# A two-layer trunk on one core: stick-breaking queries split unscaled out of PSUM, the norm factor of each token in the sigmoids

## The chip, the cores and the metric

The kernel runs on one core of one Trainium2 chip. The time is that of one execution on the device, in microseconds. Three runs of the kernel before gave 2856.43, 2856.97 and 2860.07 us, a median of 2856.97 us. The core has TensorE (matmuls, PE in the profile, its weight loads PEld), VectorE (DVE), ScalarE (ACT), GpSimd (POOL) and SyncE (SP), which work side by side and meet at semaphores. Each takes its instructions in the order in which they were written. TensorE writes to PSUM, which has 8 banks of 128 x 512 float32.

## The reference

Two layers, of which the first mixes tokens by a short convolution and the second by stick-breaking attention. The change is in the second alone. Cut to what matters there:

```python
h = rmsnorm(x, g_mix[i])                      # one factor per token: rsqrt(mean(x*x) + eps)
p0, p1, p2 = split(h @ w_in[i])               # queries, keys, values of 16 heads of 64
z = einsum(q, k) * 64 ** -0.5                 # keys before the query's own place only
log_keep = log_sigmoid(-z)
a = exp(log_sigmoid(z) + sum of log_keep over the later keys)
o = a @ v
```

The factor of a token multiplies all of its query. So it can be put on the query, or on the row of z that belongs to the query. The kernel works on sigmoids in place of logarithms: keep = sigmoid(-z), a running product of keep from the last key to the first, times sigmoid(z).

## The kernel before

Activations lie with features on the partitions and the 1024 tokens along the row. To keep float32 precision each operand of a large product is split into a rounded part (hi) and what is left (lo), and three matmuls are made of one (`three`, lines 1756 to 1758).

The stick-breaking layer goes head pair by head pair, 8 pairs. `pair` exists on every engine and has 8 items: item `it` is query block `t = it % 4` (256 tokens) of head `it // 4` of the pair. Two rows `r` of 128 queries make up an item. For one row TensorE computes z into banks 0 to 3 (`z`, lines 1985 to 1987, the last matmul of it adds the mask), ScalarE takes both sigmoids from there (lines 960 and 961), VectorE forms the running product (`scan`, line 1440), GpSimd multiplies the two (`weigh`, line 658). In the next item TensorE transposes the result into banks 4 and 5 (`turn`, line 2027), ScalarE and VectorE split it (lines 986 and 1482), and TensorE multiplies it with the values (`weighted`, lines 2043 and 2044). ScalarE and VectorE add up the two halves of the output (lines 1010 and 1528).

In the same loop TensorE computes the queries, keys and values of the next pair, `hp + 1`: six pieces of 8 steps of three matmuls, pieces 0 and 1 the query halves (tokens 0 to 511 and 512 to 1023), 2 and 3 the keys, 4 and 5 the values. All six go through one bank, number 7, one after the other (`project`, line 1989). The table `FILL` says how many steps stand behind each row of z and each part of `weighted`:

```python
FILL = [(3, 3), (2, 2, 2), (4, 1, 1, 1), (0, 2, 1, 1, 1), (3, 3), (2, 2, 2), (4, 2, 1, 1), (0, 4, 0, 0, 0)]
```

So piece 0 ends behind z of row 0 in item 1, `(1, 0)`, and piece 1 behind z of row 0 in item 2, `(2, 0)`. The first step of piece 2 stands right behind z of row 1 in item 2, and waits until bank 7 has been emptied. `ENDS` holds the six places, and VectorE empties the bank there (`project`, line 1442): for queries it multiplies with 1/8 and the norm factors R into the buffer `tf` (line 1456), for the rest with R alone (line 1236). Later ScalarE rounds `tf` into `sq` or `sk` (line 972) and VectorE subtracts (`lo_part`, line 1469). For the queries both stand at the end of items 1 and 2.

`head_place` gives the slots of `sq`: the first head of every pair has slot 0. So the queries of the next pair are written over those that this pair's items 0 to 3 read. z of item 3 is computed in item 2, and reads tokens 768 to 1023 of slot 0.

Pair 0 and pair 7 stand alone in the program, pairs 1 to 6 are a loop of three turns with two pairs each. Pair 7 has no projection in it.

Of the kernel before, what the change touches and what calls it, by code (L numbers as in the profile page):

```python
# [27 lines left out]
P = 128  # L28
# [57 lines left out]
def trunk(nc, xT, memT, wpack, vectors, out):  # L86
# [6 lines left out]
    for i in range(LAYERS):  # L93
# [3 lines left out]
        u, f, v = u + C_UNITS, f + C_UNITS, v + 2 * C_UNITS  # L97
# [13 lines left out]
    with ExitStack() as ctx:  # L111
# [50 lines left out]
        eps_r2 = place("eps_r2", [P, KB], F32)  # L162
        Z = cursor[0]
# [186 lines left out]
        zeros_made = sem("zeros_made")  # L350
        vT_full = sem("vT_full")
# [127 lines left out]
        assert len(ENDS) == 6  # L479
        ln = slice(0, HALF), slice(HALF, SEQ)  # L480
# [291 lines left out]
        def _(act):  # L772
# [101 lines left out]
            for i in range(LAYERS):  # L874
# [80 lines left out]
                else:  # L955
                    def sigmoids(row, par, r, t):
                        n = key_count(r, t)
                        act.wait_ge(z_full, row + 1)
                        z = banks(2 * r)[:, 0:n]
                        act.activation(keep[:, par, r, 0:n], z, ACT.Sigmoid, scale=-1.0).then_inc(keep_ready, 1)  # L960
                        act.activation(sig[:, par, r, 0:n], z, ACT.Sigmoid).then_inc(sig_ready, 1)  # L961

                    def project(hp, to, piece, b=7):

                        if piece < 4:
                            act.wait_ge(evacuated, hp * 6 + (v0 + piece + 1))
                            half = ln[piece % 2]
                            for other in range(1 + piece // 2):
                                for hh in range(2):
                                    slot, rows, twin = head_place(hh, to)  # L970
                                    dst = (sq, sk)[piece // 2]
                                    act.activation(dst[twin if other else rows, slot, half], tf[rows, half], ACT.Copy
# [16 lines left out]
                    def pair(hp, par, last, first=False):  # L989

                        for it in range(ITEMS):
# [3 lines left out]
                            if not (last and it == ITEMS - 1):  # L995
                                for r in range(2):
                                    sigmoids(hp * ROWS + (2 * (it + 1) + r), (it + 1) % 2, r, (it + 1) % 4)
                            if not last and it in (0, 3, 7):
# [13 lines left out]
                            if not last and it in (1, 2):  # L1012
                                project(hp + 1, 1 - par, it - 1)
# [7 lines left out]
                    act.wait_ge(x_spilled, 16)  # L1021
                    for r in range(2):
# [178 lines left out]
        def _(dve):  # L1201
# [107 lines left out]
            for i in range(LAYERS):  # L1309
# [124 lines left out]
                else:  # L1434
# [7 lines left out]
                    def project(hp, piece, b=7):  # L1442

                        part, h = piece // 2, piece % 2
                        if h == 0:
# [8 lines left out]
                        if part == 0:  # L1454

                            dve.scalar_tensor_tensor(tf[:, ln[h]], ps[:, b, :], float(SHEAD) ** -0.5,  # L1456
                                                     R[:, ln[h]], ALU.mult, ALU.mult).then_inc(evacuated, 1)
                        else:
                            scaled(tf[:, ln[h]], b, h)

                    def lo_part(hp, to, piece):
# [786 lines left out]
```

## Time and profile before

| | |
|---|---|
| three runs, median | 2856.97 us |
| the profiled execution, its own time | 2850.37 us |
| its span | 2848.8 us |
| busy: TensorE, VectorE, ScalarE, GpSimd | 2667.8, 1451.9, 1060.1, 590.7 us |
| stick-breaking stage | some 1394 to 2003 us of the span |
| one steady pair in it | 1484.05 to 1555.28 us, 71.2 us |
| mean granted clock of TensorE | 0.976 |

Busy times say which engine has most to do, and not what ends a wait. In a pipeline such as this stage the rows in time order, with the idle time in front of an instruction and what ended it, show where an engine stands still. Matmuls overlap in these rows: one of 512 columns is shown as 0.39 us long, and the next starts 0.23 us behind it. A granted clock of 1.00 is 2.4 GHz, 0.50 is 1.2 GHz.

### The profile page before, as it was taken

The numbers are of one execution on the slowest core, as the hardware profiler recorded it, in microseconds if no ns is written. First come the engines' busy times: TensorE is split into PE (matmuls) and PEld (weight loads), VectorE is DVE, ScalarE is ACT, GpSimd is POOL, SyncE is SP. The second block draws the span as 40 slices with busy tenths as digits, with TensorE's granted clock in tenths as the row PEclk, the third lists the DMA queues.
The fourth block names the chain that finished last, engine by engine and source line by source line (L and its number), as shares of the span: only waits on it lengthen the run. The fifth ranks groups of instructions, "written<-read, shape, count | busy, mean of one in ns | idle before, by whom it ended". The sixth has DMA issues, their size and how long they took to land.

```text
span 2848.8 us, 35436 instructions
## 1 busy us (share of the span) xinstructions
PE 2667.8 (94%) x12680; PEld 2220.0 (78%) x12680; DVE 1451.9 (51%) x1793; ACT 1060.1 (37%) x1749; POOL 590.7 (21%) x463
## 2 busy tenths in 40 slices
PE   7999999988999999999999889896998899999999
PEld 7888888866888878887877777775786788887887
DVE  7454434285444442334677767677328544444131
ACT  6450103243333330225666556565324333333020
POOL 2200000152222210003033333332015222221000
PEclk9999999999999999999999999998999999999999
DMA  6401111212222261103111101111321222226111
GB/s 200 141 30 44 52 52 45 88 52 89 89 103 103 77 231 51 43 34 140 54 29 30 31 23 30 30 30 61 127 88 52 103 81 96 103 81 228 51 51 69
DMA packets 57439, 221.77 MB, mean 78 GB/s; under 512 B 7280, under 2 KB 7280, under 8 KB 51824
## 3 DMA queue, kind: packets, MB, share of 16 engines
q1 hardware_dynamic: 43920, 164.68, 17.1%
q0 software_dynamic: 13120, 49.29, 5.1%
q10 hardware_dynamic: 288, 6.29, 0.5%
q8 instruction: 72, 1.18, 0.2%
q14 instruction: 39, 0.32, 0.0%
HBM read 170.43 MB, written 49.81 MB: 77 GB/s over the span
## 4 chain that ended last, share of the span: by engine, by line
PE 80%; DVE 7%; issue 5%; POOL 3%; ACT 3%; DMA 1%; POOLq 0%; SPq 0%; ACTq 0%; DVEq 0%
PE ps L1756 25%; PE ps L1758 24%; PE ps L1757 24%; POOL sig L658 2%; PE ps L2027 2%; ACT sig L961 1%; PE ps L1986 1%; PE ps L1985 1%; DVE x L1620 1%; DVE tile_lo L1629 1%; DVE w_lo L1208 1%; DVE tile_lo L1634 1%; DVE keep L1440 1%; DMA stage<-d_act 1%; PE ps L1857 1%
## 5 line engine op out<-in xcount | busy, mean ns | idle before, releaser
L1756 PE MATMUL ps<-xg_hi,w_hi 128*128 128x512 f32 x1280 | 517.2, 404 | 21.0 <-DVE tf L1456 8.4
L1757 PE MATMUL ps<-xg_lo,w_hi 128*128 128x512 f32 x1280 | 503.9, 394 | 0.0
L1758 PE MATMUL ps<-xg_hi,w_lo 128*128 128x512 f32 x1280 | 503.5, 393 | 0.0
L1756 PE MATMUL ps<-tile_hi,g_hi 128*128 128x512 f32 x1120 | 444.6, 397 | 55.6 <-DVE gate L1236 26.2
L1758 PE MATMUL ps<-tile_hi,g_lo 128*128 128x512 f32 x1120 | 441.0, 394 | 0.0
L1757 PE MATMUL ps<-tile_lo,g_hi 128*128 128x512 f32 x1120 | 439.4, 392 | 0.0
L1756 PEld LDWEIGHTS ps<-xg_hi,w_hi 128*128 128x128 f32 x1280 | 243.4, 190 | 74.2 <-DVE tf L1456 10.5
L1756 PEld LDWEIGHTS ps<-tile_hi,g_hi 128*128 128x128 f32 x1120 | 212.8, 190 | 103.0 <-issue 59.0
L1758 PEld LDWEIGHTS ps<-xg_hi,w_lo 128*128 128x128 f32 x1280 | 243.1, 190 | 53.5
L1757 PEld LDWEIGHTS ps<-xg_lo,w_hi 128*128 128x128 f32 x1280 | 243.8, 190 | 44.8 <-issue 0.7
L1756 PE MATMUL ps<-act_hi,d_hi 128*128 128x512 f32 x704 | 276.6, 393 | 0.0
L1758 PE MATMUL ps<-act_hi,d_lo 128*128 128x512 f32 x704 | 275.6, 392 | 0.0
L1757 PE MATMUL ps<-act_lo,d_hi 128*128 128x512 f32 x704 | 273.8, 389 | 0.0
L1639 DVE TENSOR_TENSOR g_lo<-quads,g_hi 128x512 fp32r<-128x512 f32 x200 | 178.9, 895 | 161.4 <-ACT g_hi L1109 161.3
L781 ACT ACTIVATE w_hi<-raw 128x1024 fp32r<-128x1024 f32 x104 | 109.8, 1058 | 398.4 <-PE ps L1758 389.9
L1758 PEld LDWEIGHTS ps<-tile_hi,g_lo 128*128 128x128 f32 x1120 | 212.5, 190 | 48.2
L1757 PEld LDWEIGHTS ps<-tile_lo,g_hi 128*128 128x128 f32 x1120 | 212.9, 190 | 46.3
L1208 DVE TENSOR_TENSOR w_lo<-raw,w_hi 128x1024 fp32r<-128x1024 f32 x104 | 139.4, 1341 | 178.2 <-ACT w_hi L781 176.4
L658 POOL TENSOR_TENSOR sig<-sig,keep 128x383 f32<-128x383 f32 (+3 forms) x121 | 167.0, 1385 | 267.2 <-DVE keep L1440 266.9
L1440 DVE TENSOR_TENSOR_SCAN keep<-keep 128x128 f32<-128x128 f32 (+7 forms) x128 | 181.7, 1433 | 52.6 <-ACT keep L960 51.9
L1715 DVE TENSOR_TENSOR x<-x,ps 128x512 f32<-128x512 f32 x64 | 43.3, 687 | 305.5 <-PE ps L1758 305.4
L1109 ACT ACTIVATE g_hi<-quads 128x512 fp32r<-128x512 f32 x200 | 125.1, 626 | 139.4 <-PE ps L1758 139.4
(212 smaller groups left out, 4130.9 us busy)
## 6 DMA issues: line engine op xcount, KB each, us to landing
raw<-wpack SPq DMA_DIRECT2D x104, 512.0 KB, 3.6
quads<-wpack SPq DMA_DIRECT2D x40, 1024.0 KB, 5.5
stage<-d_act POOLq DMA_DIRECT2D x44, 512.0 KB, 5.0
d_raw<-wpack SPq DMA_DIRECT2D x32, 704.0 KB, 4.1
d_act<-up SPq DMA_DIRECT2D x40, 256.0 KB, 2.1
d_act<-gate SPq DMA_DIRECT2D x40, 256.0 KB, 2.1
d_x<-x SPq DMA_DIRECT2D x16, 512.0 KB, 6.1
x<-d_x SPq DMA_DIRECT2D x16, 512.0 KB, 3.8
```

The source lines that it names most:

```text
L658: pool.tensor_tensor(sig[:, par, r, 0:n - 1], sig[:, par, r, 0:n - 1], keep[:, par, r, 1:n], ALU.mult).then_inc(a_ready, 1)
L781: act.activation(w_hi[s][:], raw[s][:], ACT.Copy).then_inc(w_hi_ready, 1)
L961: act.activation(sig[:, par, r, 0:n], z, ACT.Sigmoid).then_inc(sig_ready, 1)
L1109: act.activation(g_hi[i][q][:].rearrange("p (a c) -> p a c", a=1), granule_source(i, c % 2, q).rearrange("p (a c) -> p a c", a=1), ACT.Cop ...
L1208: dve.tensor_tensor(w_lo[s][:], raw[s][:], fp(w_hi[s][:]), ALU.subtract).then_inc(w_lo_ready, 1)
L1440: dve.tensor_tensor_scan(k, k, k, 1.0, ALU.mult, ALU.bypass).then_inc(scanned, 1)
L1639: dve.tensor_tensor(g_lo[i][q][:], granule_source(i, c % 2, q), fp(g_hi[i][q][:]), ALU.subtract).then_inc(g_lo_ready, 1)
L1715: dve.tensor_tensor(x[:, m, ln[h]], x[:, m, ln[h]], ps[:, (6 + 2 * m) % 8 + h, :], ALU.add).then_inc(x_added, 1)
L1756: pe.matmul(out, whi, mhi, start=start, stop=False, skip_group_check=chained)
L1757: pe.matmul(out, whi, mlo, start=False, stop=False, skip_group_check=chained)
L1758: return pe.matmul(out, wlo, mhi, start=False, stop=stop, skip_group_check=chained)
L2027: last = pe.transpose(ps[:, 4 + n % 2, j * P:(j + 1) * P], sig[:, it % 2, r, k * P:(k + 1) * P], ident[:])
```

## The change

The queries are no longer scaled. `R` and 1/8 go into `q_scale`, two columns per block of 128 tokens (+ and -), made once before the pairs by two VectorE instructions of 128 x 8. Both sigmoids take their scale from it, one number per query row, where they had a constant. For pieces 0 and 1 VectorE's multiplication into `tf` is gone: ScalarE rounds straight out of bank 7, and VectorE subtracts out of bank 7. Both now stand where `QUERIES` says: behind the sigmoids (ScalarE) and the scan (VectorE) of row 0 in item 1, and of row 1 in item 2. TensorE waits before pieces 1 and 2 for the subtraction, where it waited for the multiplication. The counts of `evacuated` follow from this (4 for a pair, not 6).

```diff
+        q_scale = place("q_scale", [P, 2, KB], F32)
...
+        QUERIES = {(1, 0): 0, (2, 1): 1}
...
-                        act.activation(keep[:, par, r, 0:n], z, ACT.Sigmoid, scale=-1.0).then_inc(keep_ready, 1)
-                        act.activation(sig[:, par, r, 0:n], z, ACT.Sigmoid).then_inc(sig_ready, 1)
+                        tok = 2 * t + r
+                        act.activation(keep[:, par, r, 0:n], z, ACT.Sigmoid, scale=q_scale[:, 1, tok:tok + 1]
+                                       ).then_inc(keep_ready, 1)
+                        act.activation(sig[:, par, r, 0:n], z, ACT.Sigmoid, scale=q_scale[:, 0, tok:tok + 1]
+                                       ).then_inc(sig_ready, 1)
...
                         if piece < 4:
-                            act.wait_ge(evacuated, hp * 6 + (v0 + piece + 1))
+                            if piece == 0:
+                                act.wait_ge(bank_full, hp * 3 + (f0 + 1))
+                            elif piece == 1:
+                                act.wait_ge(w_used, hp * 3 + (u0 + 1))
+                            else:
+                                act.wait_ge(evacuated, hp * 4 + (v0 + piece - 1))
...
-                                    act.activation(dst[twin if other else rows, slot, half], tf[rows, half], ACT.Copy
+                                    act.activation(dst[twin if other else rows, slot, half],
+                                                   ps[rows, b, :] if piece < 2 else tf[rows, half], ACT.Copy
                                                    ).then_inc(sqk_hi_ready, 1)
...
                                     sigmoids(hp * ROWS + (2 * (it + 1) + r), (it + 1) % 2, r, (it + 1) % 4)
+                                    if not last and (it, r) in QUERIES:
+                                        project(hp + 1, 1 - par, QUERIES[it, r])
...
-                            if not last and it in (1, 2):
-                                project(hp + 1, 1 - par, it - 1)
...
+                    act.wait_ge(q_scale_made, 2)
...
-                        if part == 0:
-
-                            dve.scalar_tensor_tensor(tf[:, ln[h]], ps[:, b, :], float(SHEAD) ** -0.5,
-                                                     R[:, ln[h]], ALU.mult, ALU.mult).then_inc(evacuated, 1)
-                        else:
-                            scaled(tf[:, ln[h]], b, h)
...
-                            dve.tensor_tensor(lo, tf[rows, half], fp(hi), ALU.subtract).then_inc(sqk_lo_ready, 1)
+                            dve.tensor_tensor(lo, tf[rows, half] if part else ps[rows, b, :], fp(hi), ALU.subtract
+                                              ).then_inc(sqk_lo_ready, 1)
...
-                                if not last and (it, n) in ENDS:
-                                    project(hp + 1, ENDS[it, n])
+                                if not last and (it, n) in QUERIES:
+                                    project(hp + 1, 1 - par, QUERIES[it, n])
+                                elif not last and ENDS.get((it, n), 0) > 1:
+                                    project(hp + 1, 1 - par, ENDS[it, n])
...
-                            if not last and it in (1, 2):
-                                lo_part(hp + 1, 1 - par, it - 1)
-
+
+                    for sign in range(2):
+                        dve.tensor_scalar(q_scale[:, sign, :], recip[:], (1, -1)[sign] * float(SHEAD) ** -0.5, None,
+                                          ALU.mult).then_inc(q_scale_made, 1)
...
                             if not first:
-                                pe.wait_ge(evacuated, hp * 6 + (v0 + piece))
                                 if piece == 0:
+                                    pe.wait_ge(evacuated, hp * 4 + v0)
                                     pe.wait_ge(vT_lo_ready, hp * 2)
+                                elif piece < 3:
+                                    pe.wait_ge(sqk_lo_ready, hp * 8 + 2 * piece)
+                                else:
+                                    pe.wait_ge(evacuated, hp * 4 + (v0 + piece - 2))
```

Two places show how instructions move. First VectorE in item 2 of the loop's first pair, before; the rows of L1440 are the scans of row 0 and row 1, L1456 empties bank 7 of piece 1, and the two L1469 split the queries of piece 1:

```order
L1438 REGISTER_ALU
L1440 SCALAR_TENSOR_TENSOR keep<-keep 128x896 [waits keep_ready]
L1448 REGISTER_ALU
L1456 SCALAR_TENSOR_TENSOR tf<-ps,R 128x512 [waits w_used]
L1438 REGISTER_ALU
L1440 SCALAR_TENSOR_TENSOR keep<-keep 128x1024 [waits keep_ready]
L1481 REGISTER_ALU
L1482 TENSOR_TENSOR aT_lo<-ps,aT_hi 128x384 [waits aT_hi_ready]
L1526 REGISTER_ALU
L1527 REGISTER_ALU [waits so_stored0]
L1528 TENSOR_TENSOR o_sum<-ps,o_low 64x256 [waits o_low_ready]
L1468 REGISTER_ALU
L1469 TENSOR_TENSOR sq<-tf,sq 64x512 [waits sqk_hi_ready]
L1468 REGISTER_ALU
L1469 TENSOR_TENSOR sq<-tf,sq 64x512 [waits sqk_hi_ready]
```


The same place now, with other line numbers (L1453 is the scan, L1480 the subtraction of the queries out of PSUM, L1494 the part of the transposed weights):

```order
L1451 REGISTER_ALU
L1453 SCALAR_TENSOR_TENSOR keep<-keep 128x896 [waits keep_ready]
L1451 REGISTER_ALU
L1453 SCALAR_TENSOR_TENSOR keep<-keep 128x1024 [waits keep_ready]
L1479 REGISTER_ALU
L1480 TENSOR_TENSOR sq<-ps,sq 64x512 [waits sqk_hi_ready]
L1479 REGISTER_ALU
L1480 TENSOR_TENSOR sq<-ps,sq 64x512 [waits sqk_hi_ready]
L1493 REGISTER_ALU
L1494 TENSOR_TENSOR aT_lo<-ps,aT_hi 128x384 [waits aT_hi_ready]
L1540 REGISTER_ALU
L1541 REGISTER_ALU [waits so_stored0]
L1542 TENSOR_TENSOR o_sum<-ps,o_low 64x256 [waits o_low_ready]
```


The instruction that emptied the bank between the two scans is gone, and the two subtractions, which stood at the end of the item, now stand behind the scan of row 1.

On TensorE the order is the same, and the semaphore in front of piece 2 is another. Before, from z of row 1 of item 3 (L1985 to L1987) to the first step of piece 2 (L1756):

```order
L1985 MATMUL ps<-sk,sq 128x512 [waits sig_ready]
L1986 MATMUL ps<-sk_lo_124,sq 128x512
L1985 MATMUL ps<-sk,sq 128x512
L1986 MATMUL ps<-sk_lo_124,sq 128x512
L1987 MATMUL ps<-mask_r,ident_r 128x128
L1995 REGISTER_ALU
L1997 REGISTER_ALU [waits w_lo_ready]
L1756 MATMUL ps<-xg_hi,w_hi_59 128x512 [waits evacuated]
L1757 MATMUL ps<-xg_lo,w_hi_59 128x512
```


And now:

```order
L2000 MATMUL ps<-sk,sq 128x512 [waits sig_ready]
L2001 MATMUL ps<-sk_lo_125,sq 128x512
L2000 MATMUL ps<-sk,sq 128x512
L2001 MATMUL ps<-sk_lo_125,sq 128x512
L2002 MATMUL ps<-mask_r,ident_r 128x128
L2010 REGISTER_ALU
L2016 REGISTER_ALU [waits w_lo_ready]
L1771 MATMUL ps<-xg_hi,w_hi_59 128x512 [waits sqk_lo_ready]
L1772 MATMUL ps<-xg_lo,w_hi_59 128x512
```


The first matmul of piece 2 waited for the count of emptied banks, and now waits for the count of split query and key parts.

On ScalarE, item 2 now, with the sigmoids of rows 0 and 1 (L964 and L966) and the two roundings of piece 1 (L983) behind them:

```order
L961 REGISTER_ALU
L964 ACTIVATE keep<-ps,q_scale 128x896 [waits z_full]
L966 ACTIVATE sig<-ps,q_scale 128x896
L961 REGISTER_ALU
L964 ACTIVATE keep<-ps,q_scale 128x1024 [waits z_full]
L966 ACTIVATE sig<-ps,q_scale 128x1024
L975 REGISTER_ALU
L983 ACTIVATE sq<-ps 64x512 [waits w_used]
L983 ACTIVATE sq<-ps 64x512
L995 REGISTER_ALU
L998 ACTIVATE aT_hi<-ps 128x384 [waits pv_done,aT_full]
```


Before, the two roundings (L972) stood behind the copy of the low half of the output, L1010, at the end of the item, and read `tf`.

## Rows read from the trace of the kernel before

**Rows 1.** The page: the chain that ended last, share of the span.

```profile
PE 80%; DVE 7%; issue 5%; POOL 3%; ACT 3%; DMA 1%; POOLq 0%; SPq 0%; ACTq 0%; DVEq 0%
```

**Rows 2.** A stretch of 70 us: busy PE, PEld, DVE, ACT, POOL; clock, DMA.

```profile
1470.00:1540.00 70.00, 63.39 (x365) 53.91 (x364) 52.71 (x64) 42.17 (x76) 25.66 (x24) 1.00 0.11 31
```

**Rows 3.** What TensorE waited for in one steady pair, 1492 to 1564 us.

```profile
PE ps L2027 <- POOL sig L658: 3.8, 5, 1.0
PE ps L1756 <- DVE tf L1456: 1.2, 2, 0.7
```

**Rows 4.** TensorE in time order there: start, length, idle before.

```profile
1502.79 0.39 PE L1985 MATMUL ps<-sk,sq 128*128 128x512 f32 x1
...
1504.43 0.50 PE L1756 MATMUL ps<-xg_hi,w_hi 128*128 128x512 f32 x1 [0.72 <-DVE tf L1456]
...
1508.48 1.09 PE L2027 MATMUL ps<-ident,sig 128*128 128x128 f32 x8
...
1514.01 0.22 PE L1987 MATMUL ps<-mask_r,ident_r 128*128 128x128 f32 x1
1514.68 0.50 PE L1756 MATMUL ps<-xg_hi,w_hi 128*128 128x512 f32 x1 [0.45 <-DVE tf L1456]
...
1518.55 0.39 PE L2043 MATMUL ps<-aT_hi,sv 128*128 128x256 f32 x1 [0.26 <-DVE aT_lo L1482]
...
1520.17 1.09 PE L2027 MATMUL ps<-ident,sig 128*128 128x128 f32 x8 [0.95 <-POOL sig L658]
```

**Rows 5.** ScalarE, VectorE and GpSimd in time order there.

```profile
1508.74 1.27 ACT L972 ACTIVATE sq<-tf 64x512 fp32r<-64x512 f32 x2
...
1514.26 1.02 ACT L960 ACTIVATE keep<-ps 128x1024 f32<-128x1024 f32 x1 [1.52 <-PE ps L1987]
...
1515.32 2.73 DVE L1440 TENSOR_TENSOR_SCAN keep<-keep 128x1024 f32<-128x1024 f32 x1 [0.69 <-ACT keep L960]
...
1518.12 2.00 POOL L658 TENSOR_TENSOR sig<-sig,keep 128x1023 f32<-128x1023 f32 x1 [2.23 <-DVE keep L1440]
...
1479.62 2.29 DVE L1440 TENSOR_TENSOR_SCAN keep<-keep 128x1024 f32<-128x1024 f32 x1 [1.27 <-ACT keep L960]
```

**Rows 6.** Groups of one shape, 1410 to 1990 us: count, busy, mean ns.

```profile
L1469 DVE TENSOR_TENSOR sk_lo<-tf,sk 64x512 fp32r<-64x512 f32 x28 | 33.0, 1177 | 0.4
...
L1469 DVE TENSOR_TENSOR sq<-tf,sq 64x512 fp32r<-64x512 f32 x28 | 19.2, 686 | 2.6 <-ACT sq L972 1.6
...
L1474 DVE TENSOR_TENSOR sv<-ps,sv 128x512 fp32r<-128x512 f32 x16 | 11.0, 686 | 9.3 <-ACT sv L977 9.3
```

**Rows 7.** Single lines, whole span: ns min/median/max. Scale a number or a pointer.

```profile
L1051 ACT ACTIVATE xg_hi<-mix_f x16: 612/616/632, 441.3 to 456.9; 128x512 fp32r<-128x512 f32 x16
...
L796 ACT ACTIVATE xg_hi<-x,gain x64: 703/709/729, 35.9 to 2141.0; 128x512 fp32r<-128x512 f32 x64
...
L946 ACT ACTIVATE me_f<-ps x32: 383/384/388, 134.4 to 1392.3; 128x256 f32<-128x256 f32 x32
...
L869 ACT ACTIVATE va_hi<-ps,mcol x8: 448/457/465, 39.3 to 88.6; 128x256 fp32r<-128x256 f32 x8
```

**Rows 8.** TensorE in time order behind two long idle stretches.

```profile
1640.46 0.90 PE L2027 MATMUL ps<-ident,sig 128*128 128x128 f32 x3 [4.97 <-issue]
...
1949.33 1.16 PE L2027 MATMUL ps<-ident,sig 128*128 128x128 f32 x8 [4.14 <-DVE sig L1505]
```

**Rows 9.** Stretches of TensorE at both places: length, busy, clock, DMA.

```profile
1639.50:1640.00 0.50, 0.00 (x0) 0.62 0.00 0
1640.00:1640.50 0.50, 0.04 (x1) 0.50 0.04 16
1646.00:1646.50 0.50, 0.50 (x3) 0.55 0.00 0
...
1950.00:1951.00 1.00, 1.00 (x6) 0.62 0.80 119
1953.00:1954.00 1.00, 1.00 (x6) 0.68 1.03 414
```

More of the change, by code:

```diff
@@ L96, in trunk @@
         base["C", i] = (u, f, v)
-        u, f, v = u + C_UNITS, f + C_UNITS, v + 2 * C_UNITS
+        u, f, v = u + C_UNITS, f + C_UNITS, v + (6, 4)[i % 2] * KB
         base["E", i] = (u, f, v)
@@ L350, in trunk @@
         zeros_made = sem("zeros_made")
+        q_scale_made = sem("q_scale_made")
         vT_full = sem("vT_full")
@@ L1440, in scan, with project @@
                         dve.tensor_tensor_scan(k, k, k, 1.0, ALU.mult, ALU.bypass).then_inc(scanned, 1)
-                    def project(hp, piece, b=7):
+                    def project(hp, to, piece, b=7):
                         part, h = piece // 2, piece % 2
+                        if part == 0:
+                            lo_part(hp, to, piece, b)
+                            return
                         if h == 0:
@@ L1453, in project, with lo_part @@
                             dve.wait_ge(sqk_hi_ready, hp * 12 + (8 + 4 * h))
-                        if part == 0:
-                            dve.scalar_tensor_tensor(tf[:, ln[h]], ps[:, b, :], float(SHEAD) ** -0.5,
-                                                     R[:, ln[h]], ALU.mult, ALU.mult).then_inc(evacuated, 1)
-                        else:
-                            scaled(tf[:, ln[h]], b, h)
-                    def lo_part(hp, to, piece):
+                        scaled(tf[:, ln[h]], b, h)
+                    def lo_part(hp, to, piece, b=7):
                         part, half = piece // 2, ln[piece % 2]
@@ L1535, in _ @@
                             prep(u0 + 2 + piece // 2)
-                        project(0, piece, piece)
+                        project(0, 0, piece, piece)
                         if piece == 2:
@@ L1539, in _ @@
                             dve.memset(fp(sk_lo[1][0:SHEAD, :]), 0.0).then_inc(zeros_made, 1)
-                        if piece < 4:
+                        if piece in (2, 3):
                             lo_part(0, 0, piece)
@@ L2007, in turn_values @@
                     def turn_values(hp, n, b0=7):
-                        pe.wait_ge(evacuated, hp * 6 + (v0 + 6))
+                        pe.wait_ge(evacuated, hp * 4 + (v0 + 4))
                         if n == 1 and b0 == 7:
```

## The prediction

> **What bounds the kernel now.** I read the page's chain first, then stretches, then the waits of one head pair, then that pair in time order. TensorE holds 80% of the chain [rows 1], and in the steady part of the stick-breaking stage it is busy for 63.4 of 70 us, VectorE for 52.7 and ScalarE for 42.2 [rows 2]. So what ScalarE or VectorE save is worth nothing by itself. It counts only where TensorE stands still. In one pair TensorE waits 3.8 us in five places for the last product of GpSimd before a transpose (L2027), and 1.2 us in two places for VectorE to empty bank 7 of the query pieces (L1456) [rows 3]. The second is what the change could take away: 0.72 us in front of piece 1 and 0.45 us in front of piece 2 [rows 4].
>
> In time order item 2 of that pair runs like this. Transposes start at 1508.48, z of row 1 ends with the mask at 1514.01, piece 2 starts at 1514.68, the next transposes at 1520.17 after 0.95 us of idling for GpSimd [rows 4]. Meanwhile ScalarE starts on z of row 1 at 1514.26, VectorE scans it from 1515.32, GpSimd multiplies from 1518.12 [rows 5].
>
> **The change part by part.** The stage has seven pairs with a projection. The terms are for one of them first.
>
> *The wait in front of piece 2.* This is the term that decides. The old wait ended when VectorE had emptied the bank, behind the scan of row 0. The new one ends when VectorE has done two subtractions behind the scan of row 1. TensorE cannot go past it: behind it stand the rest of the projection steps, all of `weighted` of item 2, one more set of transposes, and the transposes of item 3, for which everyone waits. The order is forced by the data, too. The first head of every pair uses slot 0, so piece 1 may only be written when z of row 1 of item 3 has been computed from the old queries.
>
> When does it end? The same wait in item 1 first. Bank 7 is full when z of row 1 starts, 1502.79 [rows 4]. ScalarE needs 1.27 us for two roundings of 64x512 out of `tf` [rows 5], which I take for PSUM as well, and VectorE 0.69 us for the last subtraction [rows 6]. With the hand-overs that is about 1505.1, against 1504.43 [rows 4]. From there TensorE has no slack until the transposes at 1508.48, in front of which no idle time is shown [rows 4]. So item 2 starts 0.6 us late. Then, with 0.6 us added: ScalarE takes row 1 at 1514.9. The scan started 1.06 us behind it [rows 5]; with a scale pointer (below) 1.15 us, so at 1516.0. The scan took 2.73 us while GpSimd was at work on row 0, and 2.29 us without such company [rows 5]. Starting 0.7 us later it is nearly free of it: I take 2.3 us, until 1518.3. Two subtractions of 64x512 took 0.686 us each for the queries [rows 6]; 128x512 out of PSUM takes 0.686 us too, so I take 1.4 us for both: 1519.7. TensorE goes on at about 1519.8 in place of 1514.68. It has then stood still for 5.0 us.
>
> From there to the next transposes the old trace has 1520.17 - 0.95 - 1514.68 = 4.54 us, in which 0.26 us is a wait for the third chunk, held up then by the scan of row 1 [rows 4] and not any more. That leaves 4.28 us, and the transposes of item 3 start at 1524.1 in place of 1520.17: 3.9 us late. GpSimd is no longer the last: scanned at 1518.3, its 2.00 us [rows 5] end at 1520.4. The end of the pair is not made up later, since TensorE runs on from these transposes without a break of its own. Seven pairs: 7 x 3.9 = 27 us. The bounds: if item 2 starts on time and VectorE hands over at once, 3.2 us a pair, 22 us. The subtraction for the keys took 1177 ns in the mean [rows 6], because GpSimd ran beside it; if both new ones take that, a pair loses 1.0 us more, 34 us in all. I stay with 27, because subtractions with a PSUM operand show 686 ns.
>
> *The relief at the heads of items 2 and 3.* The two roundings of 1.27 us (from 1508.74, [rows 5]) and the two subtractions of 1.4 us stood in front of the splitting of the transposed weights. They go. But z of row 0 does not come earlier by this, and TensorE did not wait there. I count nothing. If ScalarE were the bound at the head of both items it would give back up to 1 us each, 14 us in all.
>
> *The scale as a pointer.* 16 rows of two sigmoids in each of 8 pairs, 256 instructions, had a constant as scale and now have one number per partition. No row shows a sigmoid like that. The nearest: a copy of 128x512 takes 616 ns with no scale and 709 ns with a scale pointer, a copy of 128x256 out of PSUM 384 and 457 [rows 7]. That is 73 to 93 ns. I take 0.09 us. ScalarE has the room for 256 of these (23 us over the stage), but one of them, that of keep of row 1, stands in the chain z, sigmoid, scan, product, transposes. This chain ended a wait of TensorE five times a pair [rows 3]; the wait of item 3 has just lost that role, so four: 7 x 4 x 0.09 = 2.5 us, and in pair 7, where TensorE mostly waits, 8 x 0.09 = 0.7 us. Together 3.2 us; bounds 1 us (the waits have slack of their own) and 8 us (both sigmoids of all items count). The Trainium skill's page "ScalarE: Activation LUTs", section "What ACT_TABLE_LOAD costs", says that each pointer of one number per partition adds about 93 ns, to every function alike, and that instructions back to back overlap by as much. The copies here agree at 93 ns and 73 ns; for a sigmoid no row shows it.
>
> *The clock.* In this stage TensorE does not idle for more than 1 us at a time in a steady pair [rows 3, 4], and its clock stays at 1.00 [rows 2], 2.4 GHz. After longer idling it falls to 0.50, 1.2 GHz. Behind 4.97 us of idling that ended at 1640.46 it fell at 1639.6, 4.1 us after the idling began, and stayed low for 6.8 us (0.38 of the first half microsecond, six whole ones, 0.45 at the end) [rows 8, 9]. Behind 4.14 us that ended at 1949.33 it fell at 1950.2, 5.0 us after the start, and stayed low for 3.4 us [rows 8, 9]. My new wait of 5.0 us is of this kind. A low stretch of 3.4 us that begins 4.1 to 5.0 us behind the start of the wait has 2.5 to 3.4 us of work in it, which take twice their time: 1.25 to 1.7 us lost, I take 1.4. Seven pairs: 10 us. Bounds: 0 if the clock does not fall, and 7 x 3.0 = 21 us if it is low for 6.8 us each time. The Trainium skill's page "TensorE: Matmul & The Clock Gate", section "Terms", would count the throttled time times one half, 1.7 us a pair and 12 us in all. That is more than mine, since part of a low stretch may lie in the wait, as it did at 1640.
>
> *Before the first pair.* The two VectorE instructions of 128x8 and the earlier roundings lie beside TensorE's pieces 2 to 5. The queries need no `tf` there, which may end a short wait before the first z. I give it -0.3 us and no more.
>
> The sum: 27.3 + 3.2 + 9.8 - 0.3 = 40 us. The profiled execution took 2850.37 us and would take 2890; it lay 6.6 us under the median of the runs, 2856.97, on which I put the forecast: 2897 us.
>
> **The rivals.**
>
> *The clock stays up.* Everything else as above: 30 us, 2887 us. For it speaks that idling of 0.9 us never did harm. Against it, that both idle stretches of 4 to 5 us in rows 8 were followed by a fall.
>
> *The clock stays low for the long time.* 27.3 + 3.2 + 21 - 0.3 = 51 us, 2908 us. For it, the fall at 1639.6. Against it, that there the work behind the idling was broken by another pause, while here dense projection steps follow, as at 1949.
>
> *The wait is hidden, and the kernel gets faster.* If VectorE's second subtraction of piece 1 were done when TensorE comes to piece 2, the 1.2 us of rows 3 would go in seven pairs, -8.4 us, less 3.2 for the pointers: 2852 us. It decides at the point where TensorE leaves the mask of z of row 1, 1514.6 with the shift. ScalarE cannot have taken that row, nor VectorE scanned it, by then; the order of both engines puts the splitting of piece 1 behind it. It would have to come 5 us earlier than the rows allow.
>
> *ScalarE is the bound at the heads.* Then the relief gives back up to 14 us of the 40, 2883 us. Against it speaks that no wait of TensorE for the split weights is longer than 0.26 us in item 2.
>
> **How the numbers follow.** The forecast, all terms as summed: 0.58. The clock up: 0.15. The clock low for long: 0.12. Relief at the heads: 0.10. Hidden wait: 0.03. What is left, 0.02, is that the change comes to nothing. Less than 0.2%, 6 us, cannot be told from no change in this kernel. Faster 0.03, within 0.2% 0.02, slower 0.95. The range: the low end is the smaller first term without the clock, 22 + 1 = 23 us, 2880; I put 2878. The high end holds the low clock for long and stops short of the slow subtractions on top: 2912.
>
> **What would show it.** TensorE's waits for VectorE's query subtraction in front of piece 2, seven or so, near 5 us each. Piece 1 begins with a wait of about 1.4 us. A steady pair near 76.5 us in place of 71.2. Granted clock of 0.50 for a few us in every such pair, right behind that wait. Sigmoids longer by 70 to 95 ns. No idling for GpSimd in front of the transposes of item 3. I am wrong if the wait in front of piece 2 is under 3 us, or if the pair makes up for it in items 3 to 7.

## The result, and the profile after

The changed kernel takes 2901.34 us, the median of four runs (2899.5 to 2904.21), against 2856.7 us before (four runs, 2854.33 to 2860.07). It is 1.56% slower; the ratio is 1.0156, with a 95% interval of 1.0139 to 1.0174. The forecast was 2897 us.

The profiled execution has a span of 2898.5 us, where before it was 2848.8. From the last copy ahead of the stick-breaking stage to the first rounding behind it there were 611.3 us and now 649.1. The other 12 us lie outside, in front of the stage 5 us and behind it 7 us. No changed line stands there. A second profile of the kernel before (e8, below) has 7 of these 12 too.

First, what TensorE waited for in the stage after the change (waiting line, the one waited for: total us, times, longest):

```profile
PE ps L1771 <- DVE sq L1480: 46.5, 14, 5.1
PE ps L2046 <- POOL sig L661: 23.8, 28, 2.7
```

The waits for bank 7 of the queries were 1.2 us in a pair [rows 3] and are 46.5 us in seven pairs, 6.6 us in each: 1.7 in front of piece 1 and 5.0 in front of piece 2. GpSimd is waited for in 28 places, four a pair, where it was five. Next come rows of TensorE in time order from pair 1, which answer to [rows 4]: start, length, idle before.

```profile
1514.93 0.50 PE L1771 MATMUL ps<-xg_hi,w_hi 128*128 128x512 f32 x1 [1.66 <-DVE sq L1480]
...
1518.67 1.06 PE L2046 MATMUL ps<-ident,sig 128*128 128x128 f32 x8
...
1524.21 0.22 PE L2002 MATMUL ps<-mask_r,ident_r 128*128 128x128 f32 x1
1529.41 0.79 PE L1771 MATMUL ps<-xg_hi,w_hi 128*128 128x512 f32 x1 [4.97 <-DVE sq L1480]
...
1536.02 1.07 PE L2046 MATMUL ps<-ident,sig 128*128 128x128 f32 x8
```

z of row 1 ends at the same place, its mask 5.5 us behind the transposes of item 2 as before, and the first step of piece 2 comes after 4.97 us of idling in place of 0.45. The transposes of item 3 no longer wait for GpSimd; no idle time stands in front of them. The other engines there, answering to [rows 5]:

```profile
1524.48 1.11 ACT L964 ACTIVATE keep<-ps,q_scale 128x1024 f32<-128x1024 f32 x1 [1.92 <-PE ps L2002]
...
1526.48 1.20 ACT L983 ACTIVATE sq<-ps 64x512 fp32r<-64x512 f32 x2
...
1525.62 2.29 DVE L1453 TENSOR_TENSOR_SCAN keep<-keep 128x1024 f32<-128x1024 f32 x1 [1.91 <-ACT keep L964]
1527.94 1.41 DVE L1480 TENSOR_TENSOR sq<-ps,sq 64x512 fp32r<-64x512 f32 x2
...
1527.99 1.99 POOL L661 TENSOR_TENSOR sig<-sig,keep 128x1023 f32<-128x1023 f32 x1 [2.42 <-DVE keep L1453]
```

ScalarE takes keep and sig of row 1 and then rounds piece 1. VectorE scans until 1527.9 and only then subtracts, until 1529.35. TensorE goes on at 1529.41. The scan took 2.29 us, without GpSimd beside it. GpSimd is done at 1529.98, six microseconds before TensorE comes to the transposes. The clock of TensorE at the same place, half microseconds with length, busy time, granted clock and DMA:

```profile
1528.50:1529.00 0.50, 0.00 (x0) 0.57 0.00 0
1529.00:1529.50 0.50, 0.09 (x1) 0.50 0.00 0
1534.50:1535.00 0.50, 0.50 (x3) 0.50 0.14 33
1535.00:1535.50 0.50, 0.50 (x3) 0.60 0.00 0
```

It fell at 1528.6, 4.1 us after the idling began (1524.44), and rose at 1535.4: low for 6.8 us, of which 6.0 with work. The seven pairs differ in this, though their waits are alike (5.06 us in pair 0, 4.97 in the others):

| pair | 0 | 1 | 2 | 3 | 4 | 5 | 6 |
|---|---|---|---|---|---|---|---|
| from the start of idling to the fall, us | 3.2 | 4.1 | 4.6 | 4.5 | 3.0 | 4.8 | 3.1 |
| low for, us | 6.8 | 6.8 | 3.4 | 3.4 | 6.8 | 3.4 | 6.8 |
| of that with work, us | 4.9 | 6.0 | 3.0 | 2.9 | 4.8 | 3.3 | 5.0 |
| transposes of item 2 to those of item 3, us | 16.93 | 17.35 | 15.99 | 15.92 | 16.81 | 16.10 | 16.88 |

Where the clock fell 3.0 to 4.1 us after the idling began it stayed low for 6.8 us, and where it fell at 4.5 to 4.8 us, for 3.4. The seven waits of e2 (below) show the same: 6.8 us behind falls at 2.1 to 4.1 us, 3.4 us behind those at 4.4 and 4.9. (e6, with waits of 4.5 us, has one exception, 3.4 us behind a fall at 4.0.) Nothing here shows what decides when it falls.

The price of the pointer, sigmoid of 128x1024 before (count, busy us, mean ns):

```profile
L960 ACT ACTIVATE keep<-ps 128x1024 f32<-128x1024 f32 x16 | 16.4, 1027 | 25.2 <-PE ps L1987 25.1
```

The same for the changed kernel, with the split of the queries:

```profile
L964 ACT ACTIVATE keep<-ps,q_scale 128x1024 f32<-128x1024 f32 x16 | 17.9, 1116 | 26.7 <-PE ps L2002 26.7
...
L983 ACT ACTIVATE sq<-ps x32: 577/592/594, 1398.7 to 1924.1; 64x512 fp32r<-64x512 f32 x32
...
L1480 DVE TENSOR_TENSOR sq<-ps,sq x32: 683/689/694, 1400.0 to 1925.6; 64x512 fp32r<-64x512 f32 x32
```

The sigmoid is 89 ns longer. Rounding two halves out of PSUM took 1.20 us, and out of `tf` 1.27 [rows 5]; the subtraction out of PSUM took 689 ns.

The stage is best measured from transposes to transposes. In pair 1, in us, from the first transposes of one item to those of another:

| kernel | 1 to 2 | 2 to 3 | 3 to 7 | item 7 to the next item 7 |
|---|---|---|---|---|
| before | 8.68 | 11.69 | 35.11 | 71.23 |
| changed | 9.32 | 17.35 | 35.42 | 77.96 |
| e2, constant scales | 9.23 | 16.06 | 35.03 | 76.06 |
| e3, idling filled | 9.34 | 14.60 | 35.37 | 75.18 |
| e4, split before row 1 | 9.35 | 13.42 | 35.40 | 74.02 |
| e5, second place | 9.36 | 11.58 | 35.40 | 72.18 |
| e7, that and FILL | 9.00 | 11.61 | 35.41 | 71.82 |
| e6, before, emptied late | 8.68 | 15.59 | 36.04 | 76.06 |
| e1, before, pointers | 8.79 | 11.87 | 35.66 | 72.12 |

The four pairs of the changed kernel that have no turn of the loop in them take 77.96, 76.64, 77.45 and 77.56 us, 77.4 in the mean. That is 6.2 us more than before, 43 us for seven pairs, which is the result (44.6 us by the medians) but for 1 or 2 us. The stage of the profile grew by less, 37.8 us, because its two turns of the loop happened to be shorter: the pairs with a turn in them took 10.0 us more than steady ones, together, where it was 16.0 in the profile before. What happens at the turns is told at the end.

### The profile page after: what moved, and what is told of

It reads as the page before. It is cut to its first block, busy times and chain, and to the rows that moved or that the text cites. A ratio compares the mean times of both kernels' runs of the same rounds, so it can differ in the third digit from the quotient of the medians.

```text
span 2898.5 us, 35409 instructions
## 1 busy us (share of the span) xinstructions
PE 2688.2 (93%) x12680; PEld 2234.3 (77%) x12680; DVE 1438.6 (50%) x1779; ACT 1080.1 (37%) x1749; POOL 583.4 (20%) x463
## 4 chain that ended last, share of the span: by engine, by line
PE 81%; DVE 8%; issue 5%; ACT 3%; POOL 2%; DMA 1%; SPq 0%; ACTq 0%; DVEq 0%; POOLq 0%
PE ps L1771 25%; PE ps L1772 24%; PE ps L1773 24%; PE ps L2046 2%; POOL sig L661 2%; PE ps L2001 1%; DVE x L1635 1%; PE ps L2000 1%; ACT sig L966 1%; PE ps L2062 1%; DVE tile_lo L1644 1%; ACT keep L964 1%; DVE keep L1453 1%; DVE w_lo L1221 1%; PE ps L2063 1%
## 5 line engine op out<-in xcount | busy, mean ns | idle before, releaser
L1771 PE MATMUL ps<-xg_hi,w_hi 128*128 128x512 f32 x1280 | 520.0, 406 | 59.9 <-DVE sq L1480 46.5
L661 POOL TENSOR_TENSOR sig<-sig,keep 128x383 f32<-128x383 f32 (+3 forms) x121 | 159.9, 1326 | 255.7 <-DVE keep L1453 238.2
L1453 DVE TENSOR_TENSOR_SCAN keep<-keep 128x128 f32<-128x128 f32 (+7 forms) x128 | 177.5, 1398 | 63.8 <-ACT keep L964 61.5
L1185 ACT ACTIVATE d_hi<-d_raw 128x1408 fp32r<-128x1408 f32 x32 | 44.1, 1380 | 357.0 <-PE ps L1773 338.5
```

Source lines behind the costliest of these rows:

```text
L661: pool.tensor_tensor(sig[:, par, r, 0:n - 1], sig[:, par, r, 0:n - 1], keep[:, par, r, 1:n], ALU.mult).then_inc(a_ready, 1)
L1185: act.activation(d_hi[i][t % 2][:], d_raw[i][t % 2][:], ACT.Copy).then_inc(down_hi_ready, 1)
L1453: dve.tensor_tensor_scan(k, k, k, 1.0, ALU.mult, ALU.bypass).then_inc(scanned, 1)
L1771: pe.matmul(out, whi, mhi, start=start, stop=False, skip_group_check=chained)
```

## The experiments

My theory: the place of the split makes the wait (most of the loss), the low clock behind it adds to that, and the scale pointers cost a little. The main rival: splitting out of PSUM is what costs, since two engines must read bank 7, one after the other. A rival for each part stands with it. Beside e2 to e5 the kernel before had 2855.86 us, beside e1, e6 and e7 it had 2859.02; ratios and differences to it go by these.

### e3: the idling filled with work

```diff
                                 elif piece < 3:
+                                    if piece == 2:
+                                        pe.wait_ge(aT_lo_ready, (hp - 1) * CHUNKS + (CHUNKS_BEFORE[2] + 2))
+                                        for _ in range(21):
+                                            pe.matmul(ps[:, 4, :], xg_hi[:, 0, 0:P], xg_hi[:, 0, ln[0]], start=True, stop=True)
                                     pe.wait_ge(sqk_lo_ready, hp * 8 + 2 * piece)
```

> The changed kernel with 21 more matmuls of 128x512 into bank 4, which is idle then, in front of the wait for piece 2: 4.8 us of work that nobody needs, in the place of 5.0 us of idling. Theory: the wait itself costs 3.9 us a pair by its place and stays; the low clock behind it, 3.4 to 6.8 us in each pair, costs a further 2.4 us a pair and goes. So 17 us come back: 2884 us, no granted clock of 0.50 in items 2 of the pairs with projection, transposes of item 3 3.9 us later than before and not 6.3. Rival, the low clock is free because engines other than TensorE set the pace behind the wait: 2901 us.

Measured: 2881.3 us (2879.98 to 2884.01), 20.0 us less than the changed kernel; ratio to before 1.0089 (1.0075 to 1.0103). TensorE in time order in pair 1, and then its clock:

```profile
1521.99 5.02 PE L2019 MATMUL ps<-xg_hi 128*128 128x512 f32 x21
1527.13 0.50 PE L1771 MATMUL ps<-xg_hi,w_hi 128*128 128x512 f32 x1
...
1530.99 1.06 PE L2050 MATMUL ps<-ident,sig 128*128 128x128 f32 x8
...
1520.00:1530.00 10.00, 9.88 (x50) 1.00 0.00 0
1530.00:1540.00 10.00, 10.00 (x69) 1.00 0.19 59
```

The 21 matmuls take the place of the wait, piece 2 begins just as late, and the clock stays at 1.00. Behind them the same work takes 3.86 us to the transposes; in the changed kernel it took 6.61 us. So 147 useless matmuls make the kernel faster. In the profile a steady pair is 75.3 us against 77.4, 2.1 us for the clock, 15 us in all. From item 2 to item 3 the seven pairs of the table above are 13.9 us longer than the seven here, each by 0.90 to 0.96 of half its low time with work. The medians differ by 20 us, the profiled stages by 16.8; what makes up the rest is not shown, and the turns of the loop, where TensorE never waits for "issue" in this profile, may be part of it. The low clock has a price, and the rival is out. What is left over the kernel before, 4.0 us a pair, is the wait and the pointers.

### e4: split in front of row 1

```diff
-                                    sigmoids(hp * ROWS + (2 * (it + 1) + r), (it + 1) % 2, r, (it + 1) % 4)
-                                    if not last and (it, r) in QUERIES:
-                                        project(hp + 1, 1 - par, QUERIES[it, r])
+                                    row = hp * ROWS + (2 * (it + 1) + r)
+                                    if not last and (it, r) == (2, 1):
+                                        act.wait_ge(z_full, row + 1)
+                                        project(hp + 1, 1 - par, 1)
+                                    sigmoids(row, (it + 1) % 2, r, (it + 1) % 4)
+                                    if not last and (it, r) == (1, 0):
+                                        project(hp + 1, 1 - par, 0)
```

and the same on VectorE, ahead of the scan.

> The changed kernel, but piece 1 is split in front of the sigmoids and the scan of row 1 of item 3, as soon as its z is complete. Theory: the place behind the scan makes the wait. It shrinks from 5.0 to 2.3 us, GpSimd becomes the last again at the transposes of item 3, which come 0.8 us later than before the change relative to those of item 2. With 0.6 us in item 1 and the pointers that is 13 us over the kernel before: 2870 us, or 2878 if the clock falls behind the 2.3 us too. Rival, the wait comes from reading bank 7 twice (ScalarE, then VectorE) and not from its place: it stays near 5 us, and the time near 2901.

Measured: 2877.12 us (2875.61 to 2880.76), ratio 1.0075 (1.0059 to 1.009). TensorE's waits for the query split in all pairs, and the one in front of piece 2:

```profile
PE ps L1779 <- DVE sq L1484: 27.1, 14, 2.2
...
1522.39 0.50 PE L1779 MATMUL ps<-xg_hi,w_hi 128*128 128x512 f32 x1 [2.20 <-DVE sq L1484]
```

The wait is 2.20 us and the time falls by 24 us. PSUM is read by the same two engines as in the changed kernel. The clock was low for 3.4 us behind four of the seven waits, from 2.4 to 3.4 us after the idling began, when TensorE had been at work again for 0.2 to 1.2 us. So 2.2 us of idling can be enough for a fall. The time is the one expected with the clock falling, 2878. From item 2 to item 3 it is 13.42 us in pair 1, where the clock fell, and 12.7 us in pair 2, where it did not; expected were 12.5.

### e5: a second place for the queries

```diff
+        sq3 = place("sq3", [P, 2 * P], F32R, ME + 15 * K1)
...
-        QUERIES = {(1, 0): 0, (2, 1): 1}
+        QUERIES = {(1, 0): 0, (2, 0): 1}
...
+            if hh == 0 and to == 1 and piece == 1:
+                return [(sq[:, 0], slice(a, a + 2 * P), slice(a, a + 2 * P)),
+                        (sq3, slice(0, 2 * P), slice(a + 2 * P, a + HALF))]
```

Rounding and subtraction take the place from this function, and in odd pairs z of item 3 reads its first head's queries from `sq3`.

> The changed kernel with a second place for the queries of tokens 768 to 1023 of the first head in odd pairs, so that piece 1 need not wait for z of item 3, and is split between row 0 and row 1 of item 2, where the kernel before emptied the bank. Theory: the overwriting of slot 0 is what forces the late place. The wait falls to 1.3 us, the transposes of item 3 come 11.8 us behind those of item 2 (before: 11.7), the clock stays up. What is left over the kernel before is 0.6 us in item 1 and the pointers: 2865 us. Rival, splitting out of PSUM costs by itself, by keeping bank 7 for two engines: 2880 us or more.

Measured: 2870.65 us (2866.14 to 2876.08), ratio 1.0049 (1.0032 to 1.0066). The waits of TensorE in the stage:

```profile
PE ps L2068 <- POOL sig L670: 26.1, 35, 1.0
PE ps L1792 <- DVE sq L1497: 20.2, 14, 1.7
```

Item 2 to item 3 is 11.58 us, even less than before the change, and GpSimd is waited for five times a pair again. The 5.7 us that the change had added to this interval were therefore due to the late place, with the low clock behind it, and not to the split out of PSUM; and it is the overwriting of slot 0 that forces this place. The remaining waits for bank 7 are 20.2 us (27.1 in e4), but the one in item 2 is covered by GpSimd's. What is left of the change is 0.68 us in item 1 and the pointers, 0.95 us a pair. The median is 5.7 us over the 2865 expected; the pointers are part of it (e1).

### e6: the place alone, in the kernel before

```diff
         assert len(ENDS) == 6
+        ENDS[2, 1] = ENDS.pop((2, 0))
```

> The kernel before with another part alone: VectorE empties bank 7 of piece 1 behind the scan of row 1 in item 2 and not behind that of row 0. Queries are still scaled into the buffer, nothing is split out of PSUM, all scales are constants. Theory: the place alone makes the wait. It is 4.0 to 4.5 us where it was 0.45, the transposes of item 3 come 2.9 us later, the clock falls behind it and costs up to 2.4 us more: +20 to +37 us, 2876 to 2893. Rival, the wait of the changed kernel comes from two engines reading PSUM one after the other: under +8 us here, 2864 or less.

Measured: 2896.77 us (2893.89 to 2898.19), ratio 1.013 (1.0114 to 1.0147), 38 us over the kernel before, 1 us more than the upper end of what I expected. The waits of TensorE:

```profile
PE ps L1757 <- DVE tf L1457: 36.3, 14, 4.5
PE ps L2028 <- POOL sig L659: 19.7, 28, 0.9
```

Here nothing is split out of PSUM, all scales are constants, and one instruction of 0.66 us stands behind the scan in place of two. The wait is 4.5 us and the clock falls behind all seven of them. The 36.04 us of the table, 0.93 more than before from item 3 to item 7, have another cause, since the low clock of pair 1 ends at 1528.6, ahead of item 3 (1530.69). ScalarE and VectorE at the head of item 3, and TensorE's wait for them:

```profile
1531.37 1.28 ACT L973 ACTIVATE sq<-tf 64x512 fp32r<-64x512 f32 x2
...
1532.04 1.40 DVE L1470 TENSOR_TENSOR sq<-tf,sq 64x512 fp32r<-64x512 f32 x2 [0.24 <-ACT sq L973]
...
1534.29 0.38 PE L2044 MATMUL ps<-aT_hi,sv 128*128 128x256 f32 x1 [0.47 <-DVE aT_lo L1483]
```

The split of the queries still stands at the end of item 2. Without the wait for GpSimd the transposes of item 3 come ahead of it, and it holds up the splitting of the transposed weights. From item 3 to item 4 it is 8.66 us in place of 7.68; the changed kernel, which has this split earlier, shows 7.72. That makes 6.5 of the 38 us. The other 31 us are the place and the clock behind it, most of the result. The rival, two readers of PSUM, would have given under 8 us.

### e1, e9 and e10: the pointers alone, in the kernel before

```diff
-                        act.activation(keep[:, par, r, 0:n], z, ACT.Sigmoid, scale=-1.0).then_inc(keep_ready, 1)
-                        act.activation(sig[:, par, r, 0:n], z, ACT.Sigmoid).then_inc(sig_ready, 1)
+                        act.activation(keep[:, par, r, 0:n], z, ACT.Sigmoid, scale=q_scale[:, 1, tok:tok + 1]
+                                       ).then_inc(keep_ready, 1)
+                        act.activation(sig[:, par, r, 0:n], z, ACT.Sigmoid, scale=q_scale[:, 0, tok:tok + 1]
+                                       ).then_inc(sig_ready, 1)
...
+                        dve.memset(q_scale[:, sign, :], (1.0, -1.0)[sign]).then_inc(q_scale_made, 1)
```

> The kernel before with one part of the change alone: both sigmoids take their scale from a tile that holds 1 and -1, queries are scaled and split as before. Theory: 0.09 us in the sigmoid of row 1 in the five items a pair where TensorE waits for GpSimd, and in the eight of pair 7: +4 us, 2860 over 2856, a steady pair 71.7 in place of 71.2. Rival, every sigmoid counts: +8 us or more, 2865. The other rival, no cost: 2856.

Measured: 2871.74 us (2867.32 to 2873.94), ratio 1.0042 (1.0029 to 1.0055), 12.7 us over the kernel before where I had expected 4. By the time alone the rival (every sigmoid counts, 8 us or more) fits better than my theory. The two sigmoids of 128x1024:

```profile
L963 ACT ACTIVATE keep<-ps,q_scale 128x1024 f32<-128x1024 f32 x15 | 16.8, 1117 | 22.2 <-PE ps L1995 22.2
L965 ACT ACTIVATE sig<-ps,q_scale 128x1024 f32<-128x1024 f32 x15 | 16.7, 1111 | 0.0
```

They are 0.09 us longer, as expected, but the steady pair is 0.89 us longer and not 0.45. The table shows 0.36 us of it between items 3 and 5 (15.12 where it was 14.76), where I had counted nothing since GpSimd was not the last at item 4. e9 has the pointer in keep alone, e10 in sig alone.

> The kernel before, only the sigmoid for keep (the one that the scan waits for) has its scale from a tile, here -1. With both pointers the steady pair was 72.12 us long, without 71.23. Theory: keep of row 1 is in the chain and its pointer makes most of this: 71.8 to 72.0 us from the transposes of item 7 to those of the next pair. Rival, the load of ScalarE counts, and each sigmoid alike: 71.7 here and 71.7 with the other one alone.

Each of the two has one execution, of 2868.88 us (e9) and 2861.67 us (e10), beside one of the kernel before of 2850.23; single times are not compared here, only the steady pair. The transposes of item 7 in pairs 0 and 1 of e9:

```profile
1488.70 1.09 PE L2035 MATMUL ps<-ident,sig 128*128 128x128 f32 x8 [0.95 <-POOL sig L660]
...
1560.82 1.09 PE L2035 MATMUL ps<-ident,sig 128*128 128x128 f32 x8 [0.91 <-POOL sig L660]
```

> The kernel before, only the other sigmoid (the factor that GpSimd multiplies) has its scale from a tile, here 1. Theory: it ends long before GpSimd needs it, so the pair stays at 71.2 to 71.4 us. Rival, the load of ScalarE: 71.7.

And of e10:

```profile
1487.13 1.09 PE L2035 MATMUL ps<-ident,sig 128*128 128x128 f32 x8 [0.95 <-POOL sig L660]
...
1558.66 1.09 PE L2035 MATMUL ps<-ident,sig 128*128 128x128 f32 x8 [0.83 <-POOL sig L660]
```

With keep alone the pair is 72.12 us, all of the 0.89 and more than the 71.8 to 72.0 expected. With sig alone it is 71.53, 0.30 more than before: over the 71.2 to 71.4 of my theory, under the 71.7 of the rival. The two do not add up because 0.29 us of both is the same: from the second transposes of item 3 to those of item 4 it is 4.20 us before, and 4.49 in e1, in e9 and in e10. VectorE there, first in the kernel before, then in e10:

```profile
1524.14 1.23 DVE L1208 TENSOR_TENSOR w_lo<-raw,w_hi 128x1024 fp32r<-128x1024 f32 x1
...
1527.33 1.61 DVE L1214 TENSOR_TENSOR w_lo<-raw,w_hi 128x1024 fp32r<-128x1024 f32 x1 [0.28 <-ACT w_hi L783]
```

Before, this subtraction of the next weights starts ahead of GpSimd's second short product and ends 5.20 us behind the transposes of item 3, and GpSimd's two products take 2.33 us. In e10 the product starts first, the two take 1.30 us, and the subtraction ends at 5.62 us; in e9 at 5.61 and in e1 at 5.62. The splitting of the transposed weights stands behind it, and TensorE waits. So one pointer, either of the two, is enough to turn the order round. Apart from that keep carries 0.60 us a pair and sig 0.01, as my theory had it. Of 12.7 us, 7 x 0.89 is 6.2. The profile of e1 has 6.9 us more in the stage than that of e8 and 4.3 us more behind it, where the two kernels have the same instructions; the rest stays open.

### e2: the changed kernel with constant scales

```diff
-                        act.activation(keep[:, par, r, 0:n], z, ACT.Sigmoid, scale=q_scale[:, 1, tok:tok + 1]
+                        act.activation(keep[:, par, r, 0:n], z, ACT.Sigmoid, scale=-float(SHEAD) ** -0.5
                                        ).then_inc(keep_ready, 1)
-                        act.activation(sig[:, par, r, 0:n], z, ACT.Sigmoid, scale=q_scale[:, 0, tok:tok + 1]
+                        act.activation(sig[:, par, r, 0:n], z, ACT.Sigmoid, scale=float(SHEAD) ** -0.5
                                        ).then_inc(sig_ready, 1)
```

> The changed kernel, but both sigmoids take 1/8 and -1/8 as a constant scale (the norm factor of each token is left out, so the output is another one). Theory: a scale pointer costs 0.09 us in each sigmoid, and only the one of row 1 in items where TensorE waits for GpSimd is in the chain, so 3 us come back: 2898 us where the changed kernel has 2901. Rival A, the pointer costs nothing that shows: 2901. Rival B, both sigmoids of every item count: 8 us or more come back, 2893 or less. The wait in front of piece 2 shrinks by about 0.1 us, to 4.9, and the clock still falls.

Measured: 2898.57 us (2890.69 to 2901.58), ratio 1.014 (1.0123 to 1.0156). The median is where I had it, but the intervals of the two kernels overlap, and the times do not decide between the theory and its rivals. The profile has 35.03 us from item 3 to item 7 where the changed kernel has 35.42: 0.39 us, near to the four times 0.09 of the forecast. In item 2 the clock happened to be low for 3.4 us and not 6.8, so that the whole pair says nothing on pointers.

### e7: does it reach the kernel before?

```diff
-        FILL = [(3, 3), (2, 2, 2), (4, 1, 1, 1), ...
+        FILL = [(3, 3), (2, 0, 4), (4, 0, 2, 1), ...
```

This is put on e5.

> The kernel with the second place for queries, and the table FILL changed in items 1 and 2, so that the first product with the values stands in front of pieces 1 and 2 and covers part of both waits. Theory: transposes of item 2 come 8.9 us behind those of item 1 (9.4 without the table, 8.7 in the kernel before), item 3 stays bound by GpSimd: 3 us less than without it, 2867 where that had 2870. It does not get below the kernel before, since the pointers stay and splitting out of the bank is later than emptying it. Rival, both waits are in the chain in full: 8 us or more come back, 2862, and the kernel before is reached.

Measured: 2868.15 us (2859.02 to 2871.33), ratio 1.0033 (1.002 to 1.0047). TensorE's waits for the query split fall from 20.2 to 10.3 us:

```profile
PE ps L1792 <- DVE sq L1497: 10.3, 14, 1.1
```

Item 1 to 2 goes from 9.36 to 9.00 us, item 2 to 3 does not move, since GpSimd ends there. This is the best version with unscaled queries that I have, and it is still slower than the kernel before.

### e8: the kernel before once more

> The kernel before once more, for the parts outside the stage. Between the last copy before the stage and its end the first profile has 611.3 us, before the stage 1392.3 and behind it 841. The five other profiles have 1396 to 1399 before the stage. Theory: that is scatter between executions, and another profile of the same kernel has up to 5 us more outside and 611 inside. Rival, the changed kernels are slower outside too: 1392 and 841 again.

One profiled run of 2861.64 us. It has 1397.2 us in front of the stage, 615.3 in it, and 843.8 behind it to the end of the last matmul (before: 1392.3, 611.3, 841.4). Its steady pair is 71.23 us, the same to the hundredth. So the profile on which I forecast was a short one, and the 5 us in front of the stage are scatter. Behind the stage it has less than the changed kernel's 848.2. But e2, with the changed kernel's instructions there, has 845.4, and e1, with those of the kernel before, 848.1. That speaks for scatter here as well; single profiles do not put the rival quite out.

## Why the prediction was right

*The wait in front of piece 2: right, to 0.1 us.* Forecast were 5.0 us, a scan of 2.3 us without GpSimd beside it, 0.6 us lost in item 1, and GpSimd no longer the last at item 3. Measured were 4.97, 2.29, 0.64, and no idle time. The cost by order alone was forecast at 3.9 us a pair; e3 shows 0.66 in item 1 and 2.91 in item 2, 3.6 us. The difference lies behind the wait: from piece 2 to the transposes 4.28 us were counted, and with the clock up it took 3.86 (e3). e5 shows that the overwriting of slot 0 forces the place, as the forecast said, and e6 that the place makes the wait.

*The relief at the heads: right.* Nothing of it came back. With the split gone from the head of item 3, the time from there to item 7 fell by 0.08 us at most (e2). The reason given holds for the kernel before alone, though. Once TensorE comes to item 3 without waiting for GpSimd, a split left at the end of item 2 costs 0.9 us a pair (e6); the change moved it and was spared that.

*The clock: right in kind, too small.* I took one low stretch of 3.4 us and 1.4 us lost a pair, 10 us. Four of the seven were 6.8 us long. e3 puts the price at 2.1 us a pair by the profile, 15 us. This is the term that was mis-sized most. I had the fall 4.1 to 5.0 us behind the start of idling, from two places, and it came at 3.0 to 4.8. In the three pairs that lie in my range with 4.5 us or more the low stretch was the 3.4 us that I had taken; in the four with 4.1 us or less it was 6.8 us, with 4.8 to 6.0 us of work in it. The two places of [rows 9] already were one of each, 4.1 us with 6.8 and 5.0 us with 3.4. My reason against the long stretch, that dense work follows at once, was wrong: it followed here, and the clock stayed low. Between e3 and the changed kernel, items 2 to 3 of pair 1 differ by 2.75 us; half of the 6.0 us with work would be 3.0. The Trainium skill's page "TensorE: Matmul & The Clock Gate", section "Terms", counts half of all throttled time, which gives 3.4 us for this stretch. The trace shows less: 0.8 us of the 6.8 lay in the wait, which makes 0.4 of the 0.65 us between 3.4 and 2.75.

*The pointers: right for one, and in the changed kernel; too small in the kernel before.* 0.09 us was forecast for an instruction and 89 ns measured; of the two copies that it went by, the one of 93 ns was near and the one of 73 ns was not. In the changed kernel 0.3 to 0.4 us a pair came from items 3 to 7, near the forecast. In the kernel before the same pointers cost 0.9 us a pair, twice the 0.45 expected there, with 0.29 of it from the turned order in item 3.

*In front of the first pair:* nothing to be seen, as forecast. The forecast was 4 us too low in the end, with the order term 2 us too high, the clock some 5 us too low, and the rest within scatter. The signs came as named, with 1.7 us in front of piece 1 for 1.4 and a steady pair of 77.4 us for 76.5. That the number is this close is in part luck: two terms erred against each other, and the turns of the loop, for which the forecast had no term, took 10 us in one profile and 16 in another.

## What to carry to other kernels

When work is moved out of an engine that is not the bound, look at what the moved piece now stands behind, and at whose bank or buffer it holds meanwhile. One saved instruction of VectorE cost TensorE a wait of 5 us in each pair because the new last reader of the bank had to stand behind a sigmoid and a scan. Ask of every in-place buffer who still reads it: here 1 KB more per partition took most of the loss away. And add to each new wait of a few microseconds the low clock behind it.

## What the runs showed of the hardware

TensorE's clock fell behind 2.2 us of idling in four of seven pairs (e4), and never behind the waits up to 1.7 us of e5. Behind alike waits of 5 us it fell anywhere from 2.1 to 4.9 us after their start (the changed kernel and e2), with 6.8 us low behind the early falls and 3.4 behind the late ones. Useless matmuls in place of idling made a kernel 20 us faster.

At a turn of the loop TensorE may stand still for 3.3 to 5.1 us and then for 1.6 to 2.4 us, with "issue" as the cause, and the clock falls for 6.8 or 10.2 us behind it. It did so at both inner turns in the profile before, at one in the changed kernel (5.1 us; the other has 2.65 us, put down to GpSimd), and at neither in the profiles of e3 and e7. Over steady pairs the two turns took 16.0 us in the profile before, 10.0 in the changed kernel, 6.9 in e3, 4.0 in e7, and 15.5 to 17.6 in the other eight. The profiled execution of e7, 2859.02 us, is 9 us under the median of its kernel. So single times and single spans can mislead by 10 us; the steady pairs of the kernel before lie between 71.23 and 71.28 us in both of its profiles.

Neither reading of PSUM was slower than that of the buffer by more than 3 ns: 592 ns against 628 for ScalarE's copy of 64x512, 689 against 686 for VectorE's subtraction.
